# Expert stage on one core: the first routing weights are made beside other work, and the down products of the last twelve expert blocks are computed early in plain fp32, spilled and reloaded

## The reference, cut to what matters

```python
eidx = jnp.take_along_axis(cidx, sel, axis=-1)          # 8 heads x 16 experts per token
g = jax.nn.softmax(top_s, axis=-1).astype(xb.dtype)
act = jax.nn.gelu(jnp.einsum('thkd,td->thk', u_table[eidx], xb), approximate=False)
return jnp.einsum('thk,thkd->td', g * act, v_table[eidx])
```

## Time and profile before

| what | value |
|---|---|
| median of 3 runs | 3754.21 us (3754.07 to 3755.61) |
| profiled execution, span | 3756.8 us |
| group 0's weight steps begin on DVE | 1363.99 us |
| they end (DVE starts `h_lo`) | 1514.64 us |
| first up product of group 0 | 1536.90 us |
| last instruction on DVE starts | 3751.66 us |

### The profile page before, as it was taken

The page is one execution under the profiler, slowest core; times in us unless marked ns, Lnnn a source line. Parts: engine busy times, 40 slices in busy tenths (PEclk is TensorE's granted clock), DMA queues, the critical chain, the costliest instruction groups (busy, mean ns, idle before and its releaser), DMA issues.

```text
span 3756.8 us, 55819 instructions
## 1 busy us (share of the span) xinstructions
PE 3476.1 (93%) x18342; PEld 2934.0 (78%) x18342; DVE 3120.6 (83%) x6003; ACT 1284.5 (34%) x1819; POOL 1693.9 (45%) x1071
## 2 busy tenths in 40 slices
PE   6899889878999727899999999999999999999998
PEld 2799768876444325788888888889889999999997
DVE  7455679963699979899999999898898888888888
ACT  6411454342122227333333333323222233223222
POOL 1222120041132310355555555565577777767774
PEclk9999999989999955899999999999999999999999
DMA  8599429953111034799999999999899999999996
GB/s 296 186 350 352 145 101 367 388 207 116 34 39 33 23 134 193 277 335 339 347 344 326 348 340 343 352 363 338 300 371 370 336 333 349 331 349 334 337 344 250
DMA packets 403105, 1035.07 MB, mean 276 GB/s; under 512 B 30826, under 2 KB 193422, under 8 KB 393650
## 3 DMA queue, kind: packets, MB, share of 16 engines
q1 hardware_dynamic: 229516, 494.81, 37.8%
q0 software_dynamic: 128880, 486.07, 35.1%
q10 hardware_dynamic: 44600, 52.98, 4.0%
HBM read 884.66 MB, written 149.08 MB: 275 GB/s over the span
## 4 chain that ended last, share of the span: by engine, by line
PE 35%; DVE 14%; DMA 7%; issue 6%; POOL 1%; ACT 0%; DVEq 0%; ACTq 0%; SPq 0%; POOLq 0%
PE p_y L2483 18%; PE p_a L2471 6%; PE p_a L2468 6%; PE p_a L2467 6%; DVE rows L2376 6%; DMA rows<-u_rows,pairsT 5%; DVE u_lo L2351 2%; DVE v_lo L2358 2%; POOL rows L2288 1%; DVE hot_w L2062 1%; DMA rows<-in_v,pairsT 1%; DVE pairsT L2364 1%; DVE g_hi L2367 1%; DVE hot_j L2058 1%; DMA w_ring<-weights_spill 0%
## 5 line engine op out<-in xcount | busy, mean ns | idle before, releaser
L2288 POOL DMA_INDIRECT rows<-in_v,pairsT x384 | 738.1, 1922 | 293.3 <-DVE h_rows L2389 199.1
L2288 POOL DMA_INDIRECT rows<-u_rows,pairsT x384 | 596.0, 1552 | 490.6 <-DVE pairsT L2376 418.4
L2468 PE MATMUL p_a<-h_lo,u_hi 128*128 128x384 f32 x2048 | 692.1, 338 | 0.0
L2467 PE MATMUL p_a<-h_hi,u_hi 128*128 128x384 f32 x2048 | 688.0, 336 | 4.1 <-DVE h_lo L2430 2.5
L2250 ACT ACTIVATE v_hi<-v_raw 128x1024 fp32r<-128x1024 f32 x256 | 272.0, 1062 | 752.8 <-PE p_y L2483 743.5
L2483 PE MATMUL p_y<-v_hi,g_hi 128*128 128x512 f32 x1536 | 491.2, 401 | 7.9 <-DVE g_hi L2367 7.6
L2376 DVE CUSTOM_DVE_ANT_0 rows<-rows,h_rows 128x1024 f32<-128x1024 f32 x384 | 451.5, 1221 | 52.2 <-DMA rows<-u_rows,pairsT 51.9
L2389 DVE SCALAR_TENSOR_TENSOR h_rows<-rows,pairsT,h_rows 128x1024 f32<-128x1024 f32 x381 | 467.9, 1280 | 19.4 <-DMA rows<-in_v,pairsT 19.4
L2483 PE MATMUL p_y<-v_lo,g_hi 128*128 128x512 f32 x1536 | 479.8, 393 | 0.0
L2471 PE MATMUL p_a<-h_hi,u_lo 128*128 128x384 f32 x2048 | 400.8, 337 | 18.6 <-DVE u_lo L2351 18.6
L2467 PEld LDWEIGHTS p_a<-h_hi,u_hi 128*128 128x128 f32 x2048 | 385.4, 188 | 15.1 <-issue 4.6
(11 more groups left out here) (357 smaller groups left out, 5565.2 us busy)
## 6 DMA issues: line engine op xcount, KB each, us to landing
u_raw<-in_uT SPq DMA_DIRECT2D x256, 512.0 KB, 7.7
v_raw<-in_v SPq DMA_DIRECT2D x256, 512.0 KB, 6.4
w_ring<-weights_spill POOLq DMA_DIRECT2D x32, 1536.0 KB, 14.4
key_cols<-in_uT SPq DMA_DIRECT2D x64, 512.0 KB, 8.1
u_rows<-key_rows SPq DMA_DIRECT2D x64, 512.0 KB, 7.8
wada<-in_w_ada SPq DMA_DIRECT2D x24, 1024.0 KB, 5.7
u_rows<-pairsT ACTq DMA_DIRECT2D x48, 512.0 KB, 6.9
weights_spill<-wt SPq DMA_DIRECT2D x24, 1024.0 KB, 3.9
```

The costliest lines, as they stand in the source:

```text
L2288: pool.indirect_dma_start(rows[s][n % SLOTS][:], None, (keep.u_rows, v_rows)[g], at).then_inc(rows_in[s][n % SLOTS], 16)
L2467: nc.tensor.matmul(p_a[:, 0:GT], u_hi[s][:, k, :], h_hi[:, k, :], start=k == 0, stop=False)
L2468: nc.tensor.matmul(p_a[:, 0:GT], u_hi[s][:, k, :], h_lo[:, k, :], start=False, stop=False)
```

## The change

1. **The sparse tiles' transposes and copies, the splits of blocks 0 and 1 and the rounding of h** no longer stand ahead of the weight steps on PE and ACT. They are spread among the 96 steps, at the step numbers of three tuples. ACT's and PE's loop over the steps is written out.
2. **Down products of blocks 116 to 127 of group 1** (n = 244 to 255, `AHEAD = 12`) are computed beside the weight steps of group 0, as 8 plain fp32 matmuls of 384 columns each (no splits). From step 8 on, PE does one such matmul behind each step, and the eight of the twelfth block behind step 95. Gelu follows on ACT, which writes the result (192 KB) to DRAM through its own queue. Their u blocks use the rows buffers of slot 1, which are otherwise for gathers, and the activations of group 1 use the second half of `w_ring`.
3. **In the last 12 blocks of group 1** PE has no down product, ACT no split of u and no gelu, DVE no `u_lo`. SP loads 192 KB of `act_g` in place of 512 KB of u. `weigh` waits for that load.
4. **Sparse ranks are dealt out anew** (`ranks_after(g, j)`): with J = 128, in group 0 as before; in group 1 two ranks also at j = 0, 20, 40, 61, 81, 101, then one rank every second block from j = 116 to 122 and none after.
5. **Transfers at the start:** SP issues 3 early u blocks first; the broadcast of `gate` moves behind the weight stores. POOL loads the activations of group 1 first, gathers only rank 0 at the start, reads the first 20 blocks of weights as soon as they are stored and the last 4 after, and gathers rank 1 when all early down products are done.

```diff
+    AHEAD = w.STEPS // EVERY
+    AHEAD_AT = GROUPS * J - AHEAD
...
-    def ranks_after(j):
-
-        return min(J, j + 1 + (j >= 4) + (j >= 8))
+    def ranks_after(g, j):
+
+        whole, total = J - AHEAD * g, 2 * J - AHEAD * g
+        passed = j + 1 + min(j + 1, whole)
+        return min(J, -(-J * passed // total) + (j >= 4) + (j >= 8))
...
+            def load_ahead(i):
+                wait_count(sp, ahead_full, i - U_RING + 1)
+                sp.dma_start(u_ahead[i % U_RING], a["uT"][J - AHEAD + i]).then_inc(u_ahead_in[i % U_RING], 16)
+
+            for i in range(U_RING):
+                load_ahead(i)
...
             def load(n, j, s):
-                wait_count(sp, ulo_full, n - 1)
-                sp.dma_start(u_raw[s][:], a["uT"][j]).then_inc(u_in[s], 16)
+                if ahead(n):
...
+                    sp.wait_ge(g_full, n)
+                    sp.dma_start(act_g[s], act_dram[n - AHEAD_AT]).then_inc(ahead_in[s], 16)
...
+            for n in range(w.STEPS):
+                w.scalar(act, n, n % 2, two_banks)
+                if n in COLS_AT:
+                    token_rows(COLS_AT.index(n))
+                if n in SPLITS_AT:
+                    at = SPLITS_AT.index(n)
+                    (split, split_v)[at % 2](at // 2, at // 2, at // 2)
+                if n in ROUNDED_AT:
+                    rounded_h(H_PARTS[ROUNDED_AT.index(n)])
+                if n % EVERY == 1 and n > 2 * EVERY:
+                    gelu_ahead(n // EVERY - 2)
...
+                for k in parts:
+                    last = nc.tensor.matmul(p_ahead[i % 2], u_ahead[i % U_RING][:, k, :], h_ahead[:, k, :], start=k == 0, stop=k == KD - 1)
...
+            for n in range(w.STEPS):
+                w.tensor(pe, n, n % 2, two_banks)
+                if n in COLS_AT:
+                    token_rows(COLS_AT.index(n))
+                if n == EVERY - 1:
+                    pe.wait_ge(idx_done, 2)
+                if n >= EVERY:
+                    x = n % EVERY
+                    down_ahead(n // EVERY - 1, range(KD * x // EVERY, KD * (x + 1) // EVERY))
+            down_ahead(AHEAD - 1, range(KD))
...
             for g in range(GROUPS):
                 def down(n, j, s):
+                    if ahead(n):
+                        return
```

More of the change, by code:

```diff
@@ L2189, in blocks @@
             turns(0, done, True)
-        turns(done, J // 2 - 1, False)
+        last = J // 2 - 1 - (AHEAD // 2 if g == GROUPS - 1 else 0)
+        turns(done, last, False)
+        for k in range(last, J // 2 - 1):
+            turn(k, False)
         post(o + J - 1, J - 1, 1)
@@ L2267, in between @@
                         nc.scalar.activation(keep.dots, keep.dots, ACT.Gelu).then_inc(rows_gelu, 1)
[L2269 removed]
+                blocks(act, g, split, gelu, between=between, weights=lambda n, s: w.scalar(act, n, s, one_bank), late=split_v, opened=g == 0)
         @block.gpsimd
```

108 lines of the change are left out of this document (81 added, 27 removed).

## The result

The changed kernel takes 3721.16 us (median of four runs, 3719.77 to 3729.14) against 3754.91 us for the kernel before in the same session: a ratio of 0.9914, 95% interval 0.9900 to 0.9928. It is 34 us faster where 54 were forecast, and 1 us outside the range. The profiled execution's span fell from 3756.8 to 3718.8 us, by 38.0 us where the medians differ by 33.8; single executions of either kernel differ by 8 to 9 us.

What follows compares the result with a forecast made beforehand. PE was taken to bound group 1, DVE the weight steps, and DVE and transfers the very end. 43 - 2 + 7 + 6 = 54 us gave a 3700 us median; own range 3693 to 3707, with rivals 1 to 3 3684 to 3720.

Steps and rivals of the forecast that it cites:

- The start gives 10.1 - 2 - 1 = 7 us: Weight steps: 10.1 us from earlier DVE end, less 2 for the clock's rise and 1 for slowed stores.
- Gain 6 us: First dense blocks, from `h_lo` to up(0): 6 us gained, bounds 2 and 8.
- DVE's step 12 at 1391.8: Weight steps: the first store, queued behind loads, delays DVE's step 12 to 1391.8, where 1380.1 would be free of stalls.
- Reading 20 blocks of weights beside the last stores may slow those (3.9 us to land, 5.37 allowed): 1 us: End of the weight steps: the early weight read may slow the last stores, 1 us lost.
- Then 4.2 + 0.7 + 4.2 makes up(0) due at 16.3: First dense blocks: after down(0) at 7.2 us behind `h_lo`, up(0) follows at 16.3 us.
- Hidden: Weight steps: with its early matmul a step takes PE 1.09 us at full clock, under DVE's 1.342.
- 46 - 3 = 43: Last blocks: eleven down products removed give 46 us, less 3 us of losses, so 43 us.
- DVE is usually ahead, so about 1 us is lost: Last blocks with ranks: DVE's sums exceed PE's time for 8 blocks, costing about 1 us.
- the two-block sum, 8.8 against 8.24: Last blocks: with one rank in two blocks, DVE needs 8.8 us for two, PE 8.24.
- That `v` may land late: Last blocks: v's load may take 5.1 us, took 4.8 in group 1; 2 us lost, bounds none or 11.
- The second rival: Last blocks bound by v's load or DVE: 5.1 us a block, not 4.12; 8 us more, 3708; chance 20%.
- 2 us lost in group 1: Group 1's other 116 blocks: denser ranks cost 2 us, bounds 0 and 12 (if transfers bind).

Runs made afterwards that it cites:

- e11: Changed kernel with most start loads put behind the first weight stores and each of the first two gelus waiting only for its own spill: 3706.3 us, 0.9868 of before.
- e8: Changed kernel without the 12 early down products, their loads, gelus and spills; last 12 blocks as before: 3737.2 us, 0.9947 of before.
- e5: Changed kernel with the sums of the last six ranks working on 8 of 1024 columns, gathers kept: 3717.2 us, 0.9896 of before.
- e6: Changed kernel without the gathers of the last six ranks, their sums kept at full length: 3714.4 us, 0.9893 of before.
- e10: Changed kernel with all 128 ranks of sums done before block 244, all work kept: 3716.7 us, 0.9902 of before.
- e12: Changed kernel with start loads behind stores, each gelu waiting for its own spill, v before activations, all ranks before block 244: 3707.2 us, 0.9880 of before.
- e14: e13 with v asked for before the activations in the last 12 blocks and all ranks before block 244: 3713.7 us, 0.9898 of before.
- e7: Changed kernel with one rank more before block 244 and the last three spread over every third block: 3718.9 us, 0.9905 of before.
- e3: Changed kernel with v's load issued before that of the spilled activations in the last 12 blocks: 3716.8 us, 0.9897 of before.
- e13: e11 with the eleventh early product's matmuls moved from between the last 8 weight steps to behind them: 3710.4 us, 0.9890 of before.

## Why the prediction was wrong

- **Direction and mechanism** were right in this: faster, with most of it at the end; the clock at 1.00 in the steps; a stall of ACT's step 8 by the first store (that it came within 0.3 us is luck); down(0) 7.2 us behind `h_lo`; 27.4 us behind up(253).
- **"The start gives 10.1 - 2 - 1 = 7 us" and "Gain 6 us"** came to 2.2 us together. Three terms failed, and they add up to the 10.8 us that are missing. First, "DVE's step 12 at 1391.8" is 27.8 us behind the first step and was 30.5: 2.7 us. The stores wait for the loads in front of them, and the earlier first step didn't bring the first store forward. Second, 84 steps from step 12 on: 1392.02 + 84 x 1.342 = 1504.7, and `h_lo` came at 1511.16, 6.4 us later where 2 + 1 were allowed: 3.4 us. The failed step in it is "Reading 20 blocks of weights beside the last stores may slow those (3.9 us to land, 5.37 allowed): 1 us". The store behind the read took 9.3 us and not 3.9, and DVE stood still for 3.6 us; in e11 the same stall cost PE 6.2 us and its clock. Third, "Then 4.2 + 0.7 + 4.2 makes up(0) due at 16.3" put ACT's wait for both last spills at nothing. ACT's first gelu waited 7.39 us for them, and up(0) came at 21.0: 4.7 us. The pairs of kernels with and without this wait give it 2.8 to 3.7 us.
- **"Hidden"** for the early products held by PE's own time: 1.15 us for a step with its early matmul, where 1.09 were forecast, against DVE's 1.342. What was not hidden is what comes with them, their loads ahead of the stores and the wait for their spills. The reorder without them gained 17.4 us (e8), with them 2.2, and with a lighter start and a later wait 9.3 (e11).
- **"46 - 3 = 43"** was 36.2. The step that failed is "DVE is usually ahead, so about 1 us is lost". DVE was not ahead: at 3644.18 and 3661.40 its `v_lo` comes when PE is already waiting or about to. And the two-block sum, 8.8 against 8.24, took a rank in every second block, where two of the last blocks in a row have one: they take 6.0 and 6.2 us, 4.0 us lost on these two alone, and the three later ranks cost 6 us more. That `v` may land late was priced at 2 us; it landed in 5.7 against 5.1 allowed (and in 5.8 in group 1, from 3200 to 3500). The second rival named both and its 5.1 us a block is what was measured (5.01); the two causes are shown apart by e5, e6 and e10. What no rival had is the half clock behind each pause of about 2 us: of the 9.8 us above 11 x 4.12, PE's wait for `g_hi` is 5.8 us, and 3.6 are slow matmuls behind the two long pauses.
- **"2 us lost in group 1"** was 3.3 in the one profile and 0.6 in the second of the same kernel; its stretch varies by 8 us among kernels that don't differ there, so the term is neither confirmed nor refuted. The bound of 12 us was not reached. Six more ranks in the same blocks (e10, e12, e14) cost PE 5 to 8 us of waiting for `u_lo`, and DVE waited up to 6.2 us for gathered rows ahead of it. That fits the reason given (transfers); but DVE's own work grew there as well, by 9 us in 900 (816 to 825), and no run takes the two apart.

That e6 and e7 have steps 7 us shorter than e3 and e5 with the same program at the start, and the same sum, is the late store again: it catches step 88 in e3 and e5 (DVE loses 3.8 us) and step 92 in e6 and e7 (PE is late by 6.3 and 6.7 us); the rest are shorter first stalls. Open are what decides which store is caught, and the 6.5 us by which up(0) to up(243) differs between e11 and e13, which do the same work there.

## What to carry to other kernels

Work put into an engine's idle time brings loads, stores and waits with it, and these can cost more than the work: price each transfer that will be in flight beside one that somebody waits for, and test the move without the added work, as e8 did. An engine that ends late isn't for that the bottleneck: look whether it was stopped, and by what. And compare runs only when the same stall hits the same step. When a block gets shorter, list everything on every engine that still comes once per block, and ask how far each can run ahead; with two buffers an average over two blocks may be no bound. And an increment that another engine needs should not stand behind loads on the engine that issues them.
